# Third block's feed-forward in two phases, with seven block products per 2x2

## The chip, the cores and the metric

One core of one Trainium2 chip runs the whole program. The metric is the device time of one execution in microseconds. TensorE does the matmuls, VectorE and ScalarE the elementwise work, GpSimd some of it, and SyncE issues the transfers.

## The reference, cut to what matters

Three transformer-like blocks are applied one after another to x of shape (1, 1024 tokens, 1024 channels), all in float32. Only the end of the third block is touched: its output projection, its two layer norms and its feed-forward part.

```
def channel_mlp(h, w1, b1, w2, b2):            # w1 (1024, 4096), w2 (4096, 1024)
    return jnp.square(jax.nn.relu(h @ w1 + b1)) @ w2 + b2

x_new = deepnorm_update(x, y_l, g1, ln1_g, ln1_b)        # y_l = mixer output @ w_out
x_new = deepnorm_update(x_new, channel_mlp(modulate(x_new, sh2, sc2), w1, b1, w2, b2), g2, ln2_g, ln2_b)
# deepnorm_update(x, y, gate, g, b) = layer_norm(ALPHA * x + gate * y) * g + b
```

## The kernel before, in words

Activations are kept transposed, channels on the 128 partitions and tokens along the free axis, in two halves of 512 tokens. Each float32 product is made of three matmuls: weights and operand are each split into a rounded part (hi, made by ScalarE with a copy to the rounded type) and the rest (lo, made by VectorE with a subtraction), and hi·hi, hi·lo and lo·hi are added up in PSUM.

The stage is `chain_stage`, the same helper for all three blocks. In the third block it has N = 16 slabs of weights. A slab of the up weights (`in_w1_3`) gives 256 hidden channels: for two halves n and two row blocks m an `up_unit` does 8 x 3 matmuls of 128x512 (L1262 to L1264). ScalarE takes the result out of PSUM with bias and relu (L1457) and squares it to the hi part (L1459) and to the full square (L1461); VectorE subtracts for the lo part (L1717). A slab of the down weights (`in_w2_3`) takes these 256 hidden channels to all 1024 output channels: `down_half` does 8 output blocks of 2 x 3 matmuls for a half (L1301 to L1303), and VectorE adds each PSUM bank, times a gate, to the residual X (`drain`, L1754). So hidden values live only from one slab to the next, and never leave the chip's SBUF.

TensorE's order is written out by hand: up units of slab ch, then the down products of slab ch-1. `round_slab` (ScalarE, L1444) and `split_slab` (VectorE, L1699) prepare a whole slab of 128x2048 at once. SyncE loads a slab when the slot's last reader is done. The beginning of the stage holds the output projection and the two norms of each half (class `HalfNorm`, L823 on), with the first up units as filling. Its end is `down_last` (L1318 to L1320), then the last norm: mean, centre, squares, sums, root, scale, apply, for half 0 beside the last products and for half 1 alone at the very end.

Every engine works through its own instructions in the written order, and waits on semaphores.

## Time and profile before

| | |
|---|---|
| three runs, us | 3772.07, 3773.8, 3766.03; median 3772.07 |
| profiled execution, span from first to last instruction, us | 3772.8 |
| TensorE busy | 3631.5 us, 96%, 17008 matmuls |
| VectorE busy | 2237.2 us, 59% |
| ScalarE busy | 1233.3 us, 33% |
| GpSimd busy | 198.5 us, 5% |
| mean granted TensorE clock | 0.982 |
| moved by DMA | 225.29 MB, mean 60 GB/s |

Busy shares are means over the whole program. The profile gives no time for the profiled execution beside its span; the span lies 0.7 us above the median of the runs. In the rows, a matmul's own duration (about 0.39 us) is longer than the distance between two starts, because matmuls overlap.

### The profile page before, as it was taken

How to read it: one execution, taken by the hardware profiler on the slowest of the kernel's cores; microseconds unless marked ns; L12 is line 12 of the kernel's file. 1: busy time of each engine (PE TensorE's matmuls, PEld its weight loads, DVE VectorE, ACT ScalarE, POOL GpSimd, SP SyncE). 2: the span in 40 equal slices, each digit the busy share in tenths (PEclk: the TensorE clock that was granted, in tenths of full speed). 3: DMA queues.
4: the chain of work that ended last, by engine and by line, in shares of the span. 5: the costliest groups of instructions: out<-in, count | busy, mean ns of one | idle time of the engine just before them, and what ended most of it. 6: DMA issues, size and time to landing. Idle time of an engine off the chain costs nothing. (4 is left out here: it accounts for less than half of the span.)

```text
span 3772.8 us, 42367 instructions
## 1 busy us (share of the span) xinstructions
PE 3631.5 (96%) x17008; PEld 2942.7 (78%) x17008; DVE 2237.2 (59%) x3016; ACT 1233.3 (33%) x1789; POOL 198.5 (5%) x221
## 2 busy tenths in 40 slices
PE   8999999999998999999999999988998999999997
PEld 7977778888886877668788888867986778888885
DVE  4487577777777897454456555456355664444445
ACT  3344432222224413543322222244323462322223
POOL 0000000000003101230000000022100000000000
PEclk9999999999999999999999999999998999999999
DMA  3102111111111112120132222211222101111111
GB/s 126 45 1 90 34 45 51 51 51 50 40 51 56 62 56 53 39 90 34 45 119 94 90 90 90 89 62 46 63 59 94 41 25 65 45 45 45 45 60 53
DMA packets 68149, 225.29 MB, mean 60 GB/s; under 512 B 5565, under 2 KB 18237, under 8 KB 62706
## 3 DMA queue, kind: packets, MB, share of 16 engines
q1 hardware_dynamic: 67954, 222.58, 16.8%
q8 instruction: 136, 2.23, 0.2%
q14 instruction: 59, 0.48, 0.0%
HBM read 200.34 MB, written 13.70 MB: 57 GB/s over the span
## 5 line engine op out<-in xcount | busy, mean ns | idle before, releaser
L1262 PE MATMUL psum<-mixer_r,pairs_r 128*128 128x512 f32 x2016 | 793.8, 394 | 8.6 <-DVE gemm_input_r L1693 5.3
L1264 PE MATMUL psum<-mixer_r,pairs_r 128*128 128x512 f32 x2016 | 785.9, 390 | 0.0
L1263 PE MATMUL psum<-gemm_input_r,pairs_r 128*128 128x512 f32 x2016 | 785.8, 390 | 0.0
L1301 PE MATMUL psum<-hidden_r,pairs_r 128*128 128x512 f32 x1216 | 478.8, 394 | 13.0 <-DVE residual L1751 6.1
L1302 PE MATMUL psum<-hidden_r,pairs_r 128*128 128x512 f32 x1216 | 475.3, 391 | 0.0
L1303 PE MATMUL psum<-hidden_r,pairs_r 128*128 128x512 f32 x1216 | 475.2, 391 | 0.0
L1757 DVE TENSOR_TENSOR residual<-residual,psum 128x512 f32<-128x512 f32 x560 | 361.7, 682 | 171.4 <-PE psum L1303 144.3
L1262 PEld LDWEIGHTS psum<-mixer_r,pairs_r 128*128 128x128 f32 x2016 | 379.7, 188 | 93.3 <-issue 9.2
L1263 PEld LDWEIGHTS psum<-gemm_input_r,pairs_r 128*128 128x128 f32 x2016 | 379.7, 188 | 82.4 <-issue 4.1
L1264 PEld LDWEIGHTS psum<-mixer_r,pairs_r 128*128 128x128 f32 x2016 | 379.3, 188 | 79.2
L1699 DVE TENSOR_TENSOR pairs_r<-pairs,pairs_r 128x2048 fp32r<-128x2048 f32 (+1 forms) x108 | 223.4, 2070 | 276.5 <-ACT pairs_r L1444 276.5
L1444 ACT ACTIVATE pairs_r<-pairs 128x2048 fp32r<-128x2048 f32 (+1 forms) x108 | 187.2, 1736 | 595.6 <-DMA pairs<-in_w 376.2
L1754 DVE SCALAR_TENSOR_TENSOR residual<-psum,ada,residual 128x512 f32<-128x512 f32 x240 | 179.7, 750 | 175.5 <-PE psum L1303 166.6
L1301 PEld LDWEIGHTS psum<-hidden_r,pairs_r 128*128 128x128 f32 x1216 | 229.6, 189 | 65.1 <-DVE residual L1751 7.7
L1303 PEld LDWEIGHTS psum<-hidden_r,pairs_r 128*128 128x128 f32 x1216 | 229.5, 189 | 48.4
L1302 PEld LDWEIGHTS psum<-hidden_r,pairs_r 128*128 128x128 f32 x1216 | 229.6, 189 | 47.3 <-issue 0.2
L1717 DVE TENSOR_TENSOR hidden_r<-mixer,hidden_r 128x512 fp32r<-128x512 f32 x172 | 118.5, 690 | 103.4 <-ACT mixer L1461 82.8
L1452 ACT ACTIVATE conv_raw<-psum 128x512 f32<-128x512 f32 x88 | 52.5, 598 | 357.2 <-PE psum L1264 357.2
L2289 DVE SCALAR_TENSOR_TENSOR mixer<-scratch,params,mixer 128x1024 f32<-128x1024 f32 x120 | 157.2, 1310 | 4.1
L1726 DVE TENSOR_SCALAR mixer<-conv_raw,params 128x512 f32<-128x512 f32 x88 | 48.9, 555 | 155.5 <-ACT conv_raw L1452 155.4
L338 PE MATMUL psum<-gemm_input_r,weights_r 128*128 128x512 f32 x256 | 105.2, 411 | 10.9 <-DVE residual_r L638 10.9
L340 PE MATMUL psum<-gemm_input_r,weights_r 128*128 128x512 f32 x256 | 100.5, 392 | 0.0
(566 smaller groups left out, 5851.0 us busy)
## 6 DMA issues: line engine op xcount, KB each, us to landing
pairs<-in_w_up SPq DMA_DIRECT2D x38, 1024.0 KB, 6.9
pairs<-in_w SPq DMA_DIRECT2D x32, 1024.0 KB, 5.3
pairs<-in_w_down SPq DMA_DIRECT2D x16, 1024.0 KB, 5.2
norm_a<-in_w_ada SPq DMA_DIRECT2D x12, 1024.0 KB, 4.9
norm_b<-in_w_ada SPq DMA_DIRECT2D x12, 1024.0 KB, 5.0
pairs<-in_w_down SPq DMA_DIRECT2D x22, 512.0 KB, 3.5
pairs<-in_w_in SPq DMA_DIRECT2D x10, 1024.0 KB, 5.3
weight_slots<-in_w_in SPq DMA_DIRECT2D x9, 1024.0 KB, 4.9
```

Of the source, the lines that this page charges most:

```text
L1262: pe.matmul(out, w_hi[:, at], c.MR[:, k, halves[n]], start=k == 0, stop=False)
L1263: pe.matmul(out, w_hi[:, at], c.HR[:, k, halves[n]], start=False, stop=False)
L1264: mm = pe.matmul(out, w_lo[:, at], c.MR[:, k, halves[n]], start=False, stop=k == KT - 1)
L1301: pe.matmul(bank, hi, hid(0, ch, n, kd), start=kd == 0, stop=False)
L1302: pe.matmul(bank, lo, hid(0, ch, n, kd), start=False, stop=False)
L1303: mm = pe.matmul(bank, hi, hid(1, ch, n, kd), start=False, stop=kd == KD - 1)
L1444: act.activation(hi, src, ACT.Copy).then_inc(split_hi, 1)
L1699: dve.tensor_tensor(lo, src, hi.bitcast(F32), ALU.subtract).then_inc(split_ready, 1)
L1717: dve.tensor_tensor(hid(1, ch, n, m), mixed[n][:, m, :], hid(0, ch, n, m).bitcast(F32), ALU.subtract).then_inc(hid_ready, 1)
L1754: dve.scalar_tensor_tensor(out=x, in0=ps, scalar=gate(m), in1=x, op0=ALU.mult, op1=ALU.add).then_inc(down_drained, 1)
L1757: dve.tensor_tensor(x, x, ps, ALU.add).then_inc(down_drained, 1)
L2289: dve.scalar_tensor_tensor(out=out, in0=U[:, j:j + T], scalar=w, in1=out, op0=ALU.mult, op1=ALU.add).then_inc(taps, 1)
```

## The change

The third block calls `phased_stage` in place of `chain_stage`. Output projection, norms and the up products of the first three slabs stay as they were. After that:

- Up phase: 13 pairs. A pair is one slab (256 hidden channels) by all 1024 tokens, seen as a 2x2 of blocks in each operand, and made from seven block products in place of eight: 7 x 4 x 3 matmuls. Sums and differences of weight blocks are made by GpSimd, those of the operand once by VectorE. Four cells of results are put together by ScalarE (copy) and VectorE (add, square), and written to DRAM (`c.hidden`).
- Down phase: 20 groups. Groups 0 to 3 take 2+2 row blocks of hidden channels, groups 4 to 19 take 3+3; each group gives two output blocks by both halves from seven products of 2 x 3 or 3 x 3 matmuls. The weight sums are made by VectorE (`down_sums`), those of the hidden values by GpSimd (`operand_sums`), which are read back from DRAM. The operand blocks change after groups 3, 7, 11 and 15.
- Tail: the last 4 row blocks in the plain way, 16 x 4 x 3 matmuls.
- The residual is written to DRAM before, and added again during groups 8 to 15 (`add_residual`).

The core of the diff:

```diff
+DEPTHS = (2, 3, 3, 3, 3)
+BANK_OF = (0, 1, 0, 2, 0, 2, 0)
+OPENS = (True, True, False, True, False, False, False)
...
+            for i in range(PAIRS):                       # SyncE
+                keep(i, "11")
+                if i + 2 < PAIRS:
+                    sp.wait_ge(w_sums, 4 * (i + 2))
+                    sp.wait_ge(w_lo, SLABS + 3 * (i + 1) + 2)
+                    load_stage(i + 2)
+                if i == PAIRS - 1:
+                    sp.wait_ge(products, UP + 7 * (PAIRS - 1))
+                    load_block(0, "B22")
+                    load_block(0, "B12")
+                    load_down(0)
+                keep(i, "22")
+                keep(i, "21")
+                if i == PAIRS - 1:
+                    sp.wait_ge(products, UP + 7 * PAIRS)
+                    load_down(1)
+                keep(i, "12")
...
+            for g in range(GROUPS):                      # SyncE
+                q, j = divmod(g, 4)
+                if g:
+                    sp.wait_ge(products, DOWN + 7 * g)
+                    if g + 1 < GROUPS:
+                        load_down(g + 1)
+                if j == 0:
+                    sp.wait_ge(b_lo, 7 * (q + 1))
+                if q + 1 < CHUNKS_ and j < 2:
+                    for name in (("B22", "B12"), ("B11", "B21"))[j]:
+                        load_block(q + 1, name)
...
+            def down_group(g):                           # TensorE
+                q, j = divmod(g, 4)
+                h = depth(g)
+                pe.wait_ge(w_lo, SLABS + 3 * PAIRS + 2 * g + 1)
+                for r in range(7):
+                    if r == 2:
+                        pe.wait_ge(w_lo, SLABS + 3 * PAIRS + 2 * g + 2)
+                    if j == 0:
+                        pe.wait_ge(b_lo, 7 * q + r + 1)
...
+                    if g >= 2 and r in (0, 1, 3):
+                        drained(g - 2, {0: 6, 1: 1, 3: 5}[r])
+                    if r in (2, 4, 5, 6):
+                        drained(g, {2: 0, 4: 2, 5: 3, 6: 4}[r])
+                    product(PS[:, 3 * ((g + 1) % 2) + BANK_OF[r], :], r, h, down_high(g, DOWN_PLACE[r]), down_parts(g, DOWN_PLACE[r]),
+                            DOWN_HI, DOWN_LO).then_inc(products, 1)
...
+            for i in range(PAIRS):                       # ScalarE
+                if i + 1 < PAIRS:
+                    round_blocks(i + 1)
+                copy(i, "11", 0)
+                if i + 1 < PAIRS:
+                    round_sums(i + 1)
+                else:
+                    round_down(0, True)
+                copy(i, "21", 2)
+                if i == PAIRS - 1:
+                    round_operand(0, 0)
+                    round_operand(0, 1)
+                    round_operand(0, 2)
+                    round_down(0, False)
+                copy(i, "22", 3)
...
+            for g in range(GROUPS):                      # ScalarE
+                q, j = divmod(g, 4)
+                if q == 0:
+                    touch(g, 0)
+                if g + 1 < GROUPS and (g or q):
+                    round_down(g + 1, True)
+                if j == 3 and q + 1 < CHUNKS_:
+                    round_operand(q + 1, 0)
+                if q == 0:
+                    touch(g, 2)
+                if j == 3 and q + 1 < CHUNKS_:
+                    round_operand(q + 1, 1)
+                    round_operand(q + 1, 2)
+                if q == 0:
+                    touch(g, 3)
...
+                if g + 1 < GROUPS:
+                    round_down(g + 1, False)
+                if j == 3 and q + 1 < CHUNKS_:
+                    round_operand(q + 1, 3)
+                    round_operand(q + 1, 4)
+                    round_operand(q + 1, 5)
...
+            def operand_sums(q):                         # GpSimd
+                for name in b_landed:
+                    pool.wait_ge(b_landed[name], 16 * (q + 1))
+                pool.tensor_tensor(raw("T3"), raw("B22"), raw("B12"), ALU.subtract).then_inc(b_sums, 1)
+                pool.wait_ge(b_sums, 4 * q + 1)
+                pool.tensor_tensor(raw("T1"), raw("B12"), raw("B11"), ALU.subtract).then_inc(b_sums, 1)
+                pool.wait_ge(b_sums, 4 * q + 2)
+                pool.tensor_tensor(raw("T2"), raw("B22"), raw("T1"), ALU.subtract).then_inc(b_sums, 1)
+                pool.wait_ge(b_sums, 4 * q + 3)
+                pool.tensor_tensor(raw("T4"), raw("B21"), raw("T2"), ALU.subtract).then_inc(b_sums, 1)
...
+            def down_sums(g):                            # VectorE
+                dve.wait_ge(w2_landed[g % 2], 16 * (g // 2 + 1) + (0 if g % 2 else 16 * PAIRS))
+                part = lambda place: down_parts(g, place, 1, parts)
+                dve.tensor_tensor(part(4), part(0), part(2), ALU.subtract).then_inc(w_sums, 1)
+                dve.wait_ge(w_sums, 4 * PAIRS + 4 * g + 1)
+                dve.tensor_tensor(part(2), part(2), part(3), ALU.add).then_inc(w_sums, 1)
...
+            def low_operand(q, r):
+                h = DEPTHS[q]
+                dve.wait_ge(b_hi, 7 * q + r + 1)
+                if r in (0, 1, 6):
+                    dve.wait_ge(b_sums, 4 * (q + 1))
+                dve.tensor_tensor(block(*DOWN_LO[r], h), raw_block(q, OPERANDS[r]), block(*DOWN_HI[r], h).bitcast(F32),
+                                  ALU.subtract).then_inc(b_lo, 1)
...
+            for i in range(PAIRS):                       # VectorE
+                ahead = i + 1 < PAIRS
+                if ahead:
+                    low_blocks(i + 1, 0)
+                    low_blocks(i + 1, 1)
+                add(i, "11", 1)
+                if ahead:
+                    low_blocks(i + 1, 2)
+                else:
+                    low_operand(0, 0)
+                    low_operand(0, 1)
+                    down_sums(0)
+                    low_down(0, True)
+                    low_operand(0, 2)
+                    low_down(0, False)
+                add(i, "22", 4)
...
+            for g in range(GROUPS):                      # VectorE
+                q, j = divmod(g, 4)
+                switch = j == 3 and q + 1 < CHUNKS_
+                if g in READD:
+                    add_residual(g)
+                for r in range(7):
+                    if (g, r) in drain_at:
+                        drain(g, r)
+                    if switch and r:
+                        low_operand(q + 1, r - 1)
+                    if g + 1 < GROUPS and r == 1:
+                        down_sums(g + 1)
+                    if g + 1 < GROUPS and r == 2:
+                        low_down(g + 1, True)
+                    if g + 1 < GROUPS and r == 3:
+                        low_down(g + 1, False)
+                if switch:
+                    low_operand(q + 1, 6)
...
+                if g == GROUPS - 1:
+                    for e in range(2):
+                        dve.wait_ge(b_hi, 7 * CHUNKS_ + 3 + e)
+                        dve.tensor_tensor(tail_w_lo[e], tail_w_raw[e], tail_w_hi[e].bitcast(F32), ALU.subtract).then_inc(b_lo, 1)
+            b0, b1 = B
+            for m in range(KT):
+                drain_tail(0, m, b0)
+            b0.centre(dve)
+            b0.pairs(dve)
+            for m in range(4):
+                drain_tail(1, m, b1)
+            for k in range(KT):
+                b0.scale(dve, k)
+            for m in range(4, 8):
+                drain_tail(1, m, b1)
```

## Rows read from the trace of the kernel before

**Rows 1.** Windows of this stage, all engines: us, busy (count) each, PEclk, DMA share, GB/s
```profile
3200.00:3300.00 100.00, 100.00 (x443) 82.84 (x442) 43.76 (x48) 30.03 (x36) 0.00 (x0) 1.00 0.15 59
3500.00:3600.00 100.00, 100.00 (x443) 82.80 (x441) 41.37 (x47) 26.20 (x32) 0.00 (x0) 1.00 0.17 64
```

**Rows 2.** Window of TensorE (us, busy, count, PEclk), and two drains in a timeline of VectorE
```profile
3090.00:3680.00 590.00, 590.00 (x2604) 1.00 0.14 52
...
3670.24 0.75 DVE L1754 SCALAR_TENSOR_TENSOR residual<-psum,ada,residual 128x512 f32<-128x512 f32 x1 [0.61 <-PE psum L1303]
3671.60 0.75 DVE L1754 SCALAR_TENSOR_TENSOR residual<-psum,ada,residual 128x512 f32<-128x512 f32 x1 [0.61 <-PE psum L1303]
```

**Rows 3.** Waits of TensorE, 3060 to 3700 (last: 2920 to 3773): line, waited for, us, times, longest
```profile
PE psum L1301 <- DVE residual L1754: 2.4, 4, 1.4
PE psum L1318 <- DVE pairs_r L1699: 0.8, 1, 0.8
PE psum L1262 <- DVE gemm_input_r L1693: 5.3, 1, 5.3
```

**Rows 4.** Timeline of VectorE, single instructions and runs of several shapes
```profile
2699.91 0.42 DVE L3736 TENSOR_TENSOR pairs<-pairs,scratch 128x256 f32<-128x256 f32 x1
7.67 1.23 DVE L632 TENSOR_TENSOR weights_r<-weight_slots,weights_r 128x1024 fp32r<-128x1024 f32 x1 [6.29 <-ACT weights_r L507]
3682.92 2.29 DVE L1699 TENSOR_TENSOR pairs_r<-pairs,pairs_r 128x2048 fp32r<-128x2048 f32 x1 [6.49 <-ACT pairs_r L1444]
3695.84 0.75 DVE L1754 SCALAR_TENSOR_TENSOR residual<-psum,ada,residual 128x512 f32<-128x512 f32 x1 [0.63 <-PE psum L1320]
3696.62 0.69 DVE L900 TENSOR_TENSOR norm_a<-residual 128x512 f32<-128x512 f32 x1
```

**Rows 5.** Timeline of ScalarE, three shapes
```profile
3687.28 0.63 ACT L1459 ACTIVATE hidden_r<-mixer 128x512 fp32r<-128x512 f32 x1
29.53 1.05 ACT L507 ACTIVATE weights_r<-weight_slots 128x1024 fp32r<-128x1024 f32 x1
3688.48 1.90 ACT L1444 ACTIVATE pairs_r<-pairs 128x2048 fp32r<-128x2048 f32 x1
```

**Rows 6.** Timeline of GpSimd, adds and subtractions of three widths
```profile
2496.01 8.70 POOL L900 TENSOR_TENSOR norm_a<-norm_a,residual 128x512 f32<-128x512 f32 x6
2727.20 2.36 POOL L3291 TENSOR_TENSOR hidden_r<-mixer,hidden_r 128x1024 fp32r<-128x1024 f32 x1 [16.92 <-ACT hidden_r L3539]
```

**Rows 7.** Timeline of GpSimd and VectorE together, 2842 to 2848 and at 2548
```profile
2842.30 4.79 POOL L3291 TENSOR_TENSOR pairs_r<-pairs,pairs_r 128x2048 fp32r<-128x2048 f32 x1 [44.84 <-ACT pairs_r L3539]
2843.83 0.69 DVE L3794 TENSOR_TENSOR pairs<-psum,norm_b 128x512 f32<-128x512 f32 x1
2844.56 3.08 DVE L3796 TENSOR_TENSOR mixer<-mixer,pairs 128x512 f32<-128x512 f32 x1
2548.29 2.28 DVE L3699 TENSOR_TENSOR pairs_r<-pairs,pairs_r 128x2048 fp32r<-128x2048 f32 x1
2548.45 3.27 POOL L900 TENSOR_TENSOR norm_a<-residual 128x512 f32<-128x512 f32 x1 [15.92 <-DVE residual L920]
```

**Rows 8.** Transfers: issues, KB each, us from issue to landing (page; last: 0 to 40)
```profile
pairs<-in_w SPq DMA_DIRECT2D x32, 1024.0 KB, 5.3
pairs<-in_w_down SPq DMA_DIRECT2D x22, 512.0 KB, 3.5
residual<-in_x SPq DMA_DIRECT2D x4, 1024.0 KB, 11.3
```

**Rows 9.** Chain of waits and timeline of VectorE in the last 45 us
```profile
3732.06 3.43 PE psum L891 x8
3736.91 4.90 DVE L918 TENSOR_TENSOR residual<-residual,norm_a 128x512 f32<-128x512 f32 x8 [3.29 <-ACT norm_a L967]
3741.74 0.74 DVE L1754 SCALAR_TENSOR_TENSOR residual<-psum,ada,residual 128x512 f32<-128x512 f32 x1
3743.12 0.75 DVE L1754 SCALAR_TENSOR_TENSOR residual<-psum,ada,residual 128x512 f32<-128x512 f32 x1
```

**Rows 10.** Windows of TensorE: us, PE busy (count), PEclk, DMA share, GB/s
```profile
2918.00:2924.00 6.00, 0.72 (x5) 0.85 0.62 221
2924.00:2929.00 5.00, 5.00 (x12) 0.50 0.82 334
3060.00:3077.00 17.00, 14.61 (x53) 1.00 0.00 0
```

**Rows 11.** Waits of VectorE, 3075 to 3700: line, waited for, us, times, longest
```profile
DVE residual L1754 <- PE psum L1303: 166.6, 200, 4.1
DVE pairs_r L1699 <- ACT pairs_r L1444: 140.5, 29, 10.1
```

More of the change, by code:

```diff
@@ L89, in __init__ @@
         self.PWR = over("pairs_r", 36, [P, 12, T], F32R)
+        self.parts = over("parts", 36, [P, 15 * T])
+        self.parts_r = over("parts_r", 36, [P, 15 * T], F32R)
+        self.spread = over("spread", 8, [P, 28, T])
+        self.low_r = over("low_r", 16, [P, KT, T], F32R)
+        self.mid_r = over("mid_r", 24, [P, 4, T], F32R)
+        self.stage_rows = over("stage_rows", 26, [P, 2 * T])
+        self.tail_rows = over("tail_rows", 11, [P, 13, T])
+        self.tail_rows_r = over("tail_rows_r", 11, [P, 13, T], F32R)
+        self.tail_w = over("tail_w", 27, [P, 14, T])
+        self.tail_w_r = over("tail_w_r", 27, [P, 14, T], F32R)
+        self.hidden = nc.dram_tensor("hidden_rows", (P, 32, T), F32, kind="Internal").ap()
         self.conv_raw = over("conv_raw", 20, [P, 2, 2, HALF + 2])
@@ L827, in __init__ @@
     def __init__(self, c, s, n, spec, before, prev, x_ready, banks=None, squares_in=None, carried=(), paired=0,
-                 spilled=None, rest=None):
+                 spilled=None, rest=None, low_in=None):
+        self.low_in = low_in
         self.c, self.n, self.prev, self.x_ready = c, n, prev, x_ready
@@ L858, in hi, with lo @@
         return (self.c.XR if self.kind == "next" else self.c.MR)[:, k, self.half]
+    def lo(self, k):
+        return self.c.HR[:, k, self.half] if self.low_in is None else self.low_in(k)[:, self.half]
     def sq(self, k):
@@ L929, in low @@
         if self.lean:
-            dve.scalar_tensor_tensor(out=self.c.HR[:, k, self.half], in0=self.work(k), scalar=self.b(k),
+            dve.scalar_tensor_tensor(out=self.lo(k), in0=self.work(k), scalar=self.b(k),
                                      in1=self.hi(k).bitcast(F32), op0=ALU.add, op1=ALU.subtract).then_inc(self.s["lo_ready"], 1)
             return
-        dve.tensor_tensor(self.c.HR[:, k, self.half], self.work(k), self.hi(k).bitcast(F32),
+        dve.tensor_tensor(self.lo(k), self.work(k), self.hi(k).bitcast(F32),
                           ALU.subtract).then_inc(self.s["lo_ready"], 1)
@@ L2025, in _ @@
             drains(E, 1, range(4, 8), b1)
+            b1.centre(dve)
+            b1.pairs(dve)
+            for k in range(KT):
+                b1.scale(dve, k)
+    c.loads[:] = seen
+DEPTHS = (2, 3, 3, 3, 3)
+FIRST_ROW = [sum(2 * h for h in DEPTHS[:q]) for q in range(len(DEPTHS) + 1)]
+PHASE_SEMS = ("w_hi", "w_lo", "mix_hi", "mix_lo", "wo_done", "wo_drained", "products", "copied", "squared_y",
+              "spilled", "stage_landed", "w_sums", "added", "y_done", "t_raw", "t_hi", "t_lo", "w2_landed_1",
+              "b11_landed", "b21_landed", "b22_landed", "b12_landed", "b_sums", "b_hi", "b_lo", "x_landed",
+              "x_added")
@@ L3975, in build @@
                                              dict(kind="split", g=ada(32), b=ada(24), eps=ln_eps)],
+                                      offsets=(c.ada[:, 48:64:2], c.ada[:, 56:64:2], c.ada[:, 48:56:2]),
                                       last=dict(kind="x", g=g("ln2_g_3"), b=g("ln2_b_3"), eps=ln_eps), store=stored)),
@@ L3997, in wide_slab, with product_slabs @@
     return w.reshape(KT, P, HALF).transpose(1, 0, 2).reshape(P, KT * HALF)
+def product_slabs(w):
+    rows, out = w.reshape(-1, P, KT, P), []
+    for q, h in enumerate(DEPTHS):
+        for j in range(4):
+            of = rows[FIRST_ROW[q]:FIRST_ROW[q] + 2 * h][:, :, [j, j + 4], :]
+            out.append(of.transpose(1, 2, 0, 3).reshape(P, 4 * h * P))
+    return np.concatenate(out, axis=1)
 def down_slabs(w):
@@ L4065, in layouts @@
         "w1_3": pair_slabs(a["w1_3"][0]),
-        "w2_3": down_slabs(a["w2_3"][0]),
+        "w2_3": product_slabs(a["w2_3"][0]),
+        "w2_t_3": down_slabs(a["w2_3"][0][FIRST_ROW[-1] * P:]),
     }
```

656 lines of the change are left out of this document (655 added, 1 removed).

## The prediction

> **What bounds the kernel now.** I read the windows first: in the feed-forward of the third block TensorE is busy 100 of 100 us at full clock, VectorE about 43 and ScalarE 26 to 30, GpSimd not at all, and the transfers take 0.15 of the DMA engines [rows 1]. Then the timeline and a long window: between 3090 and 3680 there are 2604 matmuls in 590 us without a gap, one per 0.2266 us [rows 2]; I use 0.2267, since the drains behind every sixth are 1.36 us apart [rows 2]. Then TensorE's waits: 2.4 and 0.8 us in 640 [rows 3]. VectorE mostly waits for TensorE [rows 11]. So this stage costs its number of matmuls, and whatever takes its place is worth its matmuls less the waits it brings.
>
> **What is removed.** Before: 16 slabs x 192 = 3072 matmuls. After: 3 early slabs x 96 = 288; 13 pairs x 84 = 1092; 4 groups x 42 = 168; 16 groups x 63 = 1008; tail 192; together 2748. That is 324 fewer, x 0.2267 = **73.4 us**. These two waits, 3.2 us, sit at down products that are no longer there: 76.6 us of gain. This part is sure; the rest asks how much of it comes back as waits.
>
> **Prices used.** VectorE, two inputs: 0.42 us for 256 columns, 1.23 for 1024, 2.29 for 2048, so 0.55 for 384, 0.69 for 512, 0.96 for 768, 1.49 for 1280, 1.76 for 1536 (1.68 back to back), 2.16 for 1920; a drain 0.75 (0.67 back to back); a step that waits for the one before starts 0.03 after it [rows 4]. ScalarE: 0.63 for 512, 1.05 for 1024, 1.90 for 2048, so 0.85 for 768, 1.27 for 1280, 1.48 for 1536, 1.80 for 1920 [rows 5]. GpSimd: 1.45 per dependent 512-column step, 2.36 for 1024, 4.79 for 2048, so 3.5 for 1536 [rows 6, 7]. A transfer lands after 3.5 us for 512 KB and 5.3 for 1 MB, so 4.4 for 768 KB [rows 8]. A product of a pair is 12 matmuls, 2.72 us, of a group 6 (1.36) or 9 (2.04); a pair is 19.0, a group 9.5 or 14.3. From the last matmul's start to its reader I take 0.2 beyond the spacing, an estimate from matmuls of 0.39 us.
>
> **Up phase.** In a pair GpSimd needs 4 x 1.45 = 5.8 us, ScalarE about 6, VectorE about 8 of 19.0. The longest way, sums on GpSimd, then rounding (1.90), then the lo part (2.29), ends near 11.4 even where they wait for each other. Transfers: 1 MB issued near 8 lands near 13. Nothing is late; the cost is 0, all of it hidden by the other products of the pair. Before pair 0, VectorE's ten changes of the operand and ScalarE's four roundings fill the last six early units; I find 0.4 + 1.0 us of wait for the last copies: **1.4** (0 to 6).
>
> **Pair 12, where the phases meet.** Time 0 is its start. SyncE has `keep(12, "11")` ahead, which waits for product 1 (5.6) and two VectorE steps (7.1); only then go B22, B12 and the first down weights out. Three transfers of 512 KB in a row land near 11, 12.3 and 13.5. ScalarE waits in `round_down(0, True)` to 14.2, and the copy of cell 21 stands behind it: product 4, due at 10.9, starts at 14.9. GpSimd's `operand_sums(0)` are 4 x 2.5 from 12.3 to 22.5. VectorE waits for them in `low_operand(0, 0)`, then two operands (24.9), four sums (26.7); ScalarE's `round_down(0, False)` (28.0) and only then the copy of cell 22: product 5 starts at 28.7, product 6 at 31.4, end 34.1 against 19.0: **15.1** (8 to 22: with transfers of no length 3 us less for each of two waits; the upper end with GpSimd at 3 us a step).
>
> **A group without a change of operand, h = 3.** Weights for the next group can only be loaded when the group before is done, and land at 4.7. VectorE: drain 1 to 5.0, four sums x 0.58 to 7.35, drain 2 to 8.0 (needed for product 4 at 8.15), lo part 9.0, drain 3 9.65, second lo part 11.8, drain 4 12.45; product 6 was due at 12.2: 0.3 each. With the transfers of the operand blocks in the same queue I take 0.5 more in each of four groups: **4.4** with the rest. For h = 2 there are less products to hide the same: drain 4 ends at 9.8, due 8.2, so 1.75 for each of groups 1 and 2, 2.9 for group 0 (ScalarE and the late weights): **6.4**.
>
> **Groups 3, 7, 11, 15, where operands change.** Here VectorE also has seven `low_operand` of 1.7 = 11.8 us: 4.7 drains + 2.3 sums + 3.1 lo parts + 11.8 = 21.9 in a group of 14.3. In order: drain 1 5.0; `low_operand` of product 0 waits for ScalarE, which stood at the weights until 5.5 and rounds till 7.0: 8.8; sums 11.1; drain 2 11.8, so product 4 starts at 11.85 and not 8.15; operand 13.5, lo part 14.35, drain 3 15.05; product 5 then; operand 16.75, lo part 18.85, drain 4 19.5; product 6 19.55 to 21.6: +7.3. Operands 3 to 6 keep VectorE until 6.1 in the next group, whose product 2 needs drain 0 at 6.8 (+2.8), and the rest of that group then just keeps up: 10.3 with its own 0.3 wait. Group 3 has shorter products to hide it: 19.6 for 9.5, 13.0 with the next. Two of the next groups have `add_residual` at their head (1.3 each). 13.0 + 3 x 10.3 + 2.6 = **46.5** (20 to 65: the lower end is VectorE's load alone, 21.9 + 10 less 2 x 14.3 = 3.3 for each, and group 3).
>
> **GpSimd beside VectorE.** The trace shows that an elementwise VectorE step with two SBUF inputs does not run beside a two-input step of GpSimd: 512 columns took 3.08 us instead of 0.69 and ended 0.55 after GpSimd did, and GpSimd took 3.27 instead of 1.3 behind a 2.29 step; one with a PSUM input kept 0.69 [rows 7]. So drains go on, but sums and lo parts wait. `operand_sums` of 1536 columns are 4 x 3.6 = 14.5 us, in each of four chunks, from about 8.5 in group j = 1 into j = 2. The lo part of group j = 1 waits 2.4 us; in j = 2 the sums wait for up to two steps of 3.5, and come back as 3 to 4.2 us at product 4. Group 2, with its 9.5 us, loses 7.5. 7.5 + 5.5 + 2 x 6.7 = **26.4** (0 to 45). In the up phase the same waits stay under the cover of 19 us.
>
> **Tail.** The last weights' lo parts are put behind drain 6 of group 19: 15.2 + 2.3 = 17.5 against 14.3, so 3.3. At the end, root and `b0.scale` (1.4 + 4.9 us [rows 9]) had 48 matmuls, 10.9 us, beside them; now the second sums stand later, 5.4 us of matmuls remain, and four drains with adds (1.39 each [rows 9]) follow the scale: 5.0. **8.3** (2 to 12). Hidden values written and read are 34 MB more in 600 us, beside 50 GB/s used at 0.15 [rows 1]: nothing but the landing times above.
>
> **Clock.** After a wait of 5.3 us [rows 3] the granted clock was 0.50 for 5 us, 12 matmuls instead of 22 [rows 10]; after waits up to 1.4 us it stayed 1.00 [rows 10]. Pair 12 has an 11 us wait; the others are mostly under 4. I take two drops of 2.5: **5** (0 to 40).
>
> **Sum.** 1.4 + 15.1 + 4.4 + 6.4 + 46.5 + 26.4 + 8.3 + 5 = 113.5 back, 76.6 gained: 37 us slower. The profiled execution (3772.8) is the median within 0.8 us, so 3772.1 + 37 = **3809 us**.
>
> **Rivals.**
> (a) VectorE keeps up: between groups it has slack (10 of 14.3 us), and the order lets the backlog run out before a product waits. All that comes through drains 0, 2, 3 and 4 is 46.5 + 26.4 + 6.4 + 4.4 = 83.7 us; without it the time is 3725, with half of it 3767. It makes the change faster where the twenty groups together lose under 39 us, 2 us a group. For it: busy shares leave room everywhere [rows 1, 11]. Against: the queue is in order, drain 2 stands behind the sums and these behind a transfer, and nothing in the order changes that. 20%.
> (b) The mutual exclusion costs nothing, since GpSimd's steps fall where VectorE has only drains: 3809 - 26 = 3783. Against: its 14.5 us are longer than the gap between two groups' sums. 12%.
> (c) Loads land later than 4.7, being queued with each other (four of 1 MB together took 11.3 [rows 8]): each us goes almost whole into a group, 15 groups x 1.3 = 20: 3829. 12%.
> (d) The clock falls at each of the longer waits. There are about 16 of 2.5 us or more (two per change of operand, two per chunk for GpSimd), each with 2.4 us lost as in rows 10: 3809 - 5 + 38 = 3842. Against: 1.4 us didn't do it. 4%. The Trainium skill (TensorE: Matmul & The Clock Gate, HAM oscillation) says that idle gaps between bursts throttle the array again in each iteration; by that rule this case would be the forecast. The trace agrees with it for 5.3 us only.
>
> **How the numbers follow.** My own course has 52%, with a range of 3790 to 3832 from the ends of its largest terms taken against each other. The range that should hold 8 in 10 leaves out (a) beyond half (16%) and what lies beyond (d): 3764 to 3842. About 0.2% (7.5 us) can be told from no change. Faster by that is (a) from a little over half of its effect on, 16%. Within it are (a) at half effect (4%), (b) with milder changes of operand (5%) and the low end of my own course (2%), 11%. Slower is the rest, 73%.
>
> **What would show it.** TensorE's records in this stage down by 324, pairs of 19.0 us without a wait; a pair 12 near 34 us with waits of products 4 and 5 for ScalarE; groups 7, 11, 15 near 21.6 us and those behind them near 17, with TensorE waiting for VectorE's drains; VectorE sums of 384 columns at 3 us or more while GpSimd runs. Wrong would be: groups of 14.3 throughout (then a), down sums that never take longer than 0.6 us (then b), weights landing at 6 or later (then c), a mean clock well under 0.98 (then d).

## The result

| | us, median | lowest to highest | ratio to before, 95% interval |
|---|---|---|---|
| kernel before | 3772.94 | 3766.03 to 3780.87 | |
| changed kernel | 3810.11 | 3805.7 to 3814.66 | 1.0096 (1.0079 to 1.0112) |

The change makes the kernel 0.96% slower, 37.2 us by the medians; predicted were 3809 us and 37 us. The profiled executions are 40.1 us apart (3812.9 and 3772.8 us of span). Of these 4.9 lie ahead of everything that was edited: the wait of about 5 us before the third block's output projection [rows 3] ends at 2923.9 us before and at 2928.8 after, and in the kernels below between 2917.8 and 2928.8, with the same code in front of it. So 35.2 us lie behind that wait. In the 400 matmuls that follow it the work and its order are as before too, and the executions show two levels there: 9.8 to 9.9 us above 0.2267 us a matmul in the changed kernel and three of the others, 12.3 to 12.5 in the kernel before and the rest. By that the change costs some 37.7 us, close to the medians' 37.2.

These rows are from the page of the changed kernel. TensorE has 324 matmuls fewer (17008 before), VectorE 159 us more to do (2237.2 before), GpSimd 158:

```profile
span 3812.9 us, 42055 instructions
...
PE 3595.2 (94%) x16684; PEld 2901.2 (76%) x16684; DVE 2396.1 (63%) x3125; ACT 1271.7 (33%) x1779; POOL 356.4 (9%) x293
```

Its windows are, in the columns of rows 1, pairs 0 to 11, pair 12, groups 0 to 3, groups 4 to 16 and groups 17 to 19.

```profile
3113.00:3342.00 229.00, 228.38 (x1008) 189.21 (x1009) 119.63 (x109) 78.63 (x96) 77.61 (x48) 1.00 0.31 111
3342.00:3379.00 37.00, 24.64 (x88) 19.38 (x87) 14.65 (x18) 11.07 (x14) 9.43 (x4) 0.77 0.21 77
3379.00:3442.00 63.00, 42.78 (x168) 32.84 (x167) 40.30 (x42) 29.58 (x32) 14.05 (x4) 0.88 0.28 93
3442.00:3665.00 223.00, 189.23 (x758) 148.87 (x757) 181.82 (x184) 62.34 (x46) 49.12 (x12) 0.94 0.31 104
3665.00:3727.00 62.00, 59.72 (x254) 48.12 (x252) 44.93 (x52) 16.79 (x11) 0.00 (x0) 0.97 0.31 106
```

Where one engine was busy 100 of 100 us [rows 1] there is now a stage of three kinds: pairs that lose nothing, groups in which VectorE is busy 182 of 223 us and TensorE 189, and a middle where neither is. TensorE's waits say for whom, in pair 12, in the groups and in the tail:

```profile
PE psum L2359 <- ACT rows L2520: 12.4, 2, 8.0
...
PE psum L2359 <- DVE residual L2790: 53.2, 22, 8.3
PE psum L2359 <- ACT residual L2553: 3.1, 3, 1.8
...
PE psum L883 <- DVE norm_a L915: 6.5, 1, 6.5
...
PE psum L2430 <- DVE parts_r L2934: 3.1, 1, 3.1
```

L2790 is VectorE's drain, L2520 ScalarE's copy of a pair's cell. They replace the waits of 2.4 and 0.8 us in rows 3. VectorE's own waits in the groups show how little the loads have to do with it (L2753 is the first weight sum):

```profile
DVE residual L2790 <- PE psum L2361: 61.5, 47, 5.8
DVE low_r L2775 <- ACT mixer_r L2547: 9.7, 5, 2.6
...
DVE parts L2753 <- DMA parts<-in_w: 0.5, 2, 0.3
```

For each group, its length less its matmuls at 0.2267 us (9.5 us for groups 0 to 3, 14.3 for the others), worked out from the starts of the matmuls; "stage" is pair 12 to the last matmul of group 19, for which the matmuls alone need 285.7 us:

```
                p12   0    1    2    3    4    5    6    7    8    9    10   11   12   13   14   15   16   stage
changed         17.5  3.1  1.8  9.8 10.8  1.4  2.9  2.6  7.9  4.5  2.8  3.8  7.0  5.5  3.9  2.4  6.8  4.2  384.4
e1_sums_off     17.6  3.1  1.8  1.8 10.8  1.6  0.1  0.1  7.0  5.3  0.1  0.1  6.8  5.3  0.1  0.1  7.5  2.0  357.0
e2_handover     17.4  3.1  1.8  9.5  6.6  1.7  2.8  4.1  2.8  0.2  4.1  2.2  2.6  0.3  2.8  4.1  2.5  0.2  354.6
e3_meet          8.0  5.9  2.2  9.4 10.7  1.4  3.6  1.9  6.9  5.3  3.4  3.0  6.8  5.5  3.9  2.4  6.8  4.2  377.0
e6_order        17.1  1.1  0.0 10.1  5.4  3.7  0.4  7.5  1.3  2.8  2.4  8.1  1.3  2.8  2.2  8.2  1.3  1.9  363.7
e13_best         2.6  5.4  1.5  4.3  4.6  6.9  0.4  0.2  1.3  2.8  1.8  0.9  1.9  4.0  0.2  0.9  1.9  3.0  330.6
```

Where nothing near a group was edited it still moves by up to 1.8 us from one execution to the next, and the whole stage by about 3.

### The profile page after: what moved, and what is told of

Read it like the earlier page. It is cut to its first block and busy times, and to the rows that moved or that the text cites. A ratio compares the mean times of both kernels' runs of the same rounds, so it can differ in the third digit from the quotient of the medians.

```text
span 3812.9 us, 42055 instructions
## 1 busy us (share of the span) xinstructions
PE 3595.2 (94%) x16684; PEld 2901.2 (76%) x16684; DVE 2396.1 (63%) x3125; ACT 1271.7 (33%) x1779; POOL 356.4 (9%) x293
## 5 line engine op out<-in xcount | busy, mean ns | idle before, releaser
L1277 PE MATMUL psum<-mixer_r,pairs_r 128*128 128x512 f32 x1408 | 552.7, 393 | 3.4 <-ACT conv_raw L1467 1.7
L1279 PE MATMUL psum<-mixer_r,pairs_r 128*128 128x512 f32 x1408 | 548.4, 389 | 0.0
L1278 PE MATMUL psum<-gemm_input_r,pairs_r 128*128 128x512 f32 x1408 | 548.2, 389 | 0.0
L1316 PE MATMUL psum<-hidden_r,pairs_r 128*128 128x512 f32 x768 | 303.7, 395 | 10.7 <-DVE residual L1766 6.2
L1277 PEld LDWEIGHTS psum<-mixer_r,pairs_r 128*128 128x128 f32 x1408 | 264.8, 188 | 62.3 <-issue 7.3
L1278 PEld LDWEIGHTS psum<-gemm_input_r,pairs_r 128*128 128x128 f32 x1408 | 264.7, 188 | 56.7 <-issue 2.2
L1279 PEld LDWEIGHTS psum<-mixer_r,pairs_r 128*128 128x128 f32 x1408 | 264.6, 188 | 55.4
L1317 PE MATMUL psum<-hidden_r,pairs_r 128*128 128x512 f32 x768 | 300.9, 392 | 0.0
L1318 PE MATMUL psum<-hidden_r,pairs_r 128*128 128x512 f32 x768 | 300.9, 392 | 0.0
L1714 DVE TENSOR_TENSOR pairs_r<-pairs,pairs_r 128x1024 fp32r<-128x1024 f32 (+1 forms) x76 | 150.2, 1978 | 136.2 <-ACT pairs_r L1459 136.2
L1459 ACT ACTIVATE pairs_r<-pairs 128x1024 fp32r<-128x1024 f32 (+1 forms) x76 | 126.1, 1663 | 227.3 <-DMA pairs<-in_w_up 211.6
L2359 PE MATMUL psum<-mixer_r,parts_r 128*128 128x512 f32 x380 | 154.7, 407 | 41.6 <-DVE residual L2790 40.3
L1316 PEld LDWEIGHTS psum<-hidden_r,pairs_r 128*128 128x128 f32 x768 | 145.4, 189 | 43.7 <-DVE residual L1766 7.7
L2360 PE MATMUL psum<-gemm_input_r,parts_r 128*128 128x512 f32 x432 | 174.1, 403 | 0.0
L1318 PEld LDWEIGHTS psum<-hidden_r,pairs_r 128*128 128x128 f32 x768 | 145.4, 189 | 31.0
L1317 PEld LDWEIGHTS psum<-hidden_r,pairs_r 128*128 128x128 f32 x768 | 145.5, 189 | 29.7
L2361 PE MATMUL psum<-mixer_r,parts_r 128*128 128x512 f32 x380 | 152.9, 402 | 0.0
L2790 DVE SCALAR_TENSOR_TENSOR residual<-psum,ada,residual 128x512 f32<-128x512 f32 x124 | 92.2, 748 | 64.7 <-PE psum L2361 62.8
```

The costliest lines, as they stand in the source:

```text
L1277: pe.matmul(out, w_hi[:, at], c.MR[:, k, halves[n]], start=k == 0, stop=False)
L1278: pe.matmul(out, w_hi[:, at], c.HR[:, k, halves[n]], start=False, stop=False)
L1279: mm = pe.matmul(out, w_lo[:, at], c.MR[:, k, halves[n]], start=False, stop=k == KT - 1)
L1316: pe.matmul(bank, hi, hid(0, ch, n, kd), start=kd == 0, stop=False)
L1317: pe.matmul(bank, lo, hid(0, ch, n, kd), start=False, stop=False)
L1318: mm = pe.matmul(bank, hi, hid(1, ch, n, kd), start=False, stop=kd == KD - 1)
```

## The experiments

All start from the changed kernel. Differences in time are taken between ratios to the kernel before, since the runs were made on more than one occasion; each is uncertain by about 8 us, the stage lengths from the trace by about 3.

**GpSimd's sums left out.**

```diff
+                if q:
+                    for name in ("T3", "T1", "T2", "T4"):
+                        pool.memset(raw(name), 0.0).then_inc(b_sums, 1)
+                    return
```

> The changed kernel with GpSimd's four operand sums of chunks 1 to 4 replaced by four memsets of the same blocks (16 two-input steps of 1536 columns less; those sums are left out of what is computed). Theory (VectorE's weight sums and lo parts stand still while GpSimd runs a two-input step, and this comes back at product 4): groups 2, 6, 10 and 14 lose about 9.5, 2.7, 3.8 and 2.3 us less, the groups behind them some more, in all about 26 us: near 3784 us, 1.003 times the kernel before. Rival (the exclusion costs nothing, the same groups are late by VectorE's own work in order): no change, 3810 us, groups 2 and 6 as they were.

Measured 3780.18 us, 1.0021 (1.0011 to 1.003): 28 us faster. In the table it is the groups beside GpSimd's sums that change: 2, 5, 6, 9, 10, 13 and 14 lose 2.4 us together where they lost 28.2; of the others only group 16 differs by over a microsecond. The theory holds, and the rival falls. The timeline of the changed kernel at groups 5 and 6, VectorE first, then GpSimd, shows one of the four meetings:

```profile
3467.41 4.86 DVE L2766 TENSOR_TENSOR parts_r<-parts,parts_r 128x1920 fp32r<-128x1920 f32 x1
3472.19 1.40 DVE L2790 SCALAR_TENSOR_TENSOR residual<-psum,ada,residual 128x512 f32<-128x512 f32 x2
...
3479.48 0.75 DVE L2790 SCALAR_TENSOR_TENSOR residual<-psum,ada,residual 128x512 f32<-128x512 f32 x1 [1.29 <-PE psum L2361]
3480.15 3.05 DVE L2753 TENSOR_TENSOR parts<-parts 128x384 f32<-128x384 f32 x1
3483.23 0.56 DVE L2755 TENSOR_TENSOR parts<-parts 128x384 f32<-128x384 f32 x1
...
3466.75 3.50 POOL L2681 TENSOR_TENSOR spread<-parts,spread 128x1536 f32<-128x1536 f32 x1 [51.75 <-DMA parts<-hidden_rows]
3470.33 5.29 POOL L2683 TENSOR_TENSOR spread<-spread,parts 128x1536 f32<-128x1536 f32 x1
...
3479.28 3.51 POOL L2687 TENSOR_TENSOR spread<-parts,spread 128x1536 f32<-128x1536 f32 x1
```

The lo part took 4.86 us for 2.16 and the weight sum 3.05 for 0.55; GpSimd's second step took 5.29 for 3.5. Drains, with a PSUM input, kept 0.75 beside it.

**The handover cut to a third.** Edit, in `round_operand` and `low_operand` for q > 0:

```diff
+                cut = (lambda x: x) if q == 0 else (lambda x: x[:, h - 1:h, :])
```

> The changed kernel with the rounding and the lo part of each operand of chunks 1 to 4 done for one of its two or three row blocks only (the other blocks are left out of what is computed): every step, wait and order is kept, each step takes a third to a half of its time. Theory (VectorE's backlog of 11.8 us in groups 3, 7, 11 and 15 makes TensorE wait for the drains there and in the group behind): those eight groups lose 48 us together now and should lose about 20, so near 3781 us, 1.002 times the kernel before. Rival (these groups are late because loads land late or the clock is down, not because VectorE is full): no change, near 3810 us.

Measured 3779.22 us, 1.0019 (1.001 to 1.0029): 29 us faster. Groups 3, 4, 7, 8, 11, 12, 15 and 16 lose 16.9 us instead of 48.1, and the others differ by up to 1.7 either way. The work on the operands is the cause, not the loads or the clock. The edit shortens ScalarE's roundings as well as VectorE's lo parts, so it doesn't tell the two apart; that TensorE waits for VectorE's drains in these groups is in its waits above.

**The tail's order.**

```diff
+                    if g == GROUPS - 1 and r in (3, 4):
+                        e = r - 3
+                        dve.wait_ge(b_hi, 7 * CHUNKS_ + 3 + e)
+                        dve.tensor_tensor(tail_w_lo[e], tail_w_raw[e], tail_w_hi[e].bitcast(F32), ALU.subtract).then_inc(b_lo, 1)
...
-            down_tail_part(1, range(4, 8), 0)
             B[0].sums(pe)
+            down_tail_part(1, range(4, 8), 0)
             down_tail_part(1, range(4, 8), 1)
```

> The changed kernel with the lo parts of the last weights behind drains 3 and 4 of group 19 instead of behind drain 6, and the second sums of squares ahead of the first half of the tail's last down products instead of behind it. Same work. Theory: the wait of 3.1 us for these lo parts goes and that of 6.5 us for the normed output falls to about 2: 8 us less, near 3802 us. Rival: the lo parts delay drains 5 and 6 by as much and the end is set by the drains with their adds, not by the scale: no change within 2 us.

Measured 3797.45 us, 1.0067 (1.0052 to 1.0082): 11 us faster by the ratios. Of TensorE's waits in the tail two are left:

```profile
PE psum L906 <- DVE spread L927: 5.6, 1, 5.6
PE psum L883 <- DVE norm_a L915: 1.7, 1, 1.7
```

The 3.1 us are gone and 6.5 has become 1.7, which is 7.9. The tail gives more than that: from the last matmul of group 19 to the end of the execution it takes 75.4 us instead of 86.3 (the kernel before needs 74.7 for the same number of matmuls), so 10.9 us went, since the matmuls 0.43 us apart behind the waits went with them. That is the whole difference by the ratios. The theory holds, but its size was too small, and its rival falls.

**Pair 12's order.** The loads of B22, B12 and the first down weights ahead of `keep(12, "11")`; ScalarE's copies ahead of what waits for GpSimd; on VectorE:

```diff
-                    low_operand(0, 0)
-                    low_operand(0, 1)
                     down_sums(0)
                     low_down(0, True)
-                    low_operand(0, 2)
                     low_down(0, False)
                 add(i, "22", 4)
```

> The changed kernel with the steps of pair 12 in another order: the loads of B22, B12 and the first down weights ahead of keep(12, 11); ScalarE's copies of cells 21 and 22 ahead of what waits for GpSimd; VectorE's weight sums first and its operands behind the adds. Same work. Theory (pair 12 is late by 17.5 us because both copies stand behind waits for late loads and GpSimd's sums): pair 12 falls to about 20 us, the time by 15 to 17: near 3794 us. Half of it may come back in groups 0 to 2 if the operands become late there. Rival (the wait is for the data themselves, and moves to the first down product): pair 12 near 19, but the gap in front of group 0 grows by the same 15 us, no change.

Measured 3800.97 us, 1.0076 (1.0061 to 1.0091): 7.5 us faster, half of what was expected. Pair 12 lost 8.0 us instead of 17.5, and group 0 gave 2.8 of it back. ScalarE's copies no longer hold TensorE; what does now is VectorE's add for cell 22, which stands behind four weight sums that had become slow. VectorE in the timeline of this kernel:

```profile
3348.73 0.67 DVE L2754 TENSOR_TENSOR parts<-parts 128x256 f32<-128x256 f32 x1 [3.62 <-DMA parts<-in_w]
3349.43 2.50 DVE L2756 TENSOR_TENSOR parts<-parts 128x256 f32<-128x256 f32 x1
3351.97 2.50 DVE L2758 TENSOR_TENSOR parts<-parts 128x256 f32<-128x256 f32 x1
3354.51 2.45 DVE L2760 TENSOR_TENSOR parts<-parts 128x256 f32<-128x256 f32 x1
```

Three sums of 0.42 us took 2.5 each. GpSimd's four operand sums of 2.40 to 2.46 us ran from 3346.72 to 3356.67, and each of the last three sums of VectorE, which waits for the one before, ended just after a step of GpSimd did. In the changed kernel the four took 0.42 each, because VectorE itself stood until GpSimd was done. So the exclusion was hidden there by the bad order, and the better order met it.

**The waits filled.**

```diff
+            def fill(w_high, rows_, n):
+                for k in range(n):
+                    pe.matmul(PS[:, 6, :], w_high[:, 0:P], rows_[:, 0, :], start=True, stop=True, skip_group_check=True)
...
+                    if (g, r) in DOWN_FILL:
+                        fill(down_high(g, DOWN_PLACE[0]), block(*DOWN_HI[6 if j == 3 else 0], h), DOWN_FILL[g, r])
```

> The changed kernel, and 273 matmuls more, which write to an unused PSUM bank that nobody reads: they stand on TensorE's queue at the 23 places where it waits in pair 12 and groups 0 to 16 (50 in pair 12, the rest in the groups), in each place fewer than fit into the wait. In the records of the changed kernel the waits there are 68.6 us together, but pair and groups are 99 us longer than their matmuls at 0.2267 us: 30 us are matmuls 0.43 us apart behind the waits. Theory (the wait itself lowers the granted clock behind it): with the waits filled the clock stays up and most of the 30 us goes: near 3785 us, between 3780 and 3795. The same queues behind then make the waits a little longer. Rival (the lower clock has another cause, or the end is set by the other engines anyway, whose next step comes no earlier): within 3 us of 3810, or later by the matmuls that do not fit.

Measured 3806.48 us, 1.0091 (1.0075 to 1.0107): 2 us by the ratios, 3.6 by the medians, neither clear of the noise, and not 30. The matmuls added are 259, not 273: 50 in pair 12 and 209 in the groups. The granted clock did what the theory said. Its windows of pair 12 and the groups, in the columns of rows 1, had 0.77, 0.88 and 0.94 in the changed kernel:

```profile
3342.00:3379.00 37.00, 33.95 (x142) 27.24 (x141) 14.57 (x18) 12.23 (x16) 9.57 (x4) 0.95 0.22 76
3379.00:3442.00 63.00, 59.66 (x256) 47.15 (x255) 42.89 (x43) 30.73 (x33) 15.25 (x4) 1.00 0.30 104
3442.00:3665.00 223.00, 207.57 (x887) 165.65 (x886) 183.20 (x187) 61.91 (x46) 49.51 (x12) 0.99 0.29 104
```

The stage went from 384.4 to 378.2 us. The starts of the matmuls say where the rest stayed. In the changed kernel 72.6 us above 0.2267 a matmul lie in waits and 24.7 in matmuls 0.3 to 0.8 us apart (93 of them near 0.43, 19 us); the 30 us of the expectation count some 4 us too much, because a wait is counted there from the modelled end of the matmul before it. With the fillers the slow ones fell to 10.6 us, and waits and fillers together grew to 80.7. So some 14 us of slow matmuls went, 8 came back as waiting, and the lower clock cost about 6 us, uncertain by about 3. The rest was free: the time of the next drain is set on VectorE, whose load didn't change, and a faster TensorE only comes earlier to a longer wait. In group 7, which had three waits and one stretch of slow matmuls, 7.9 us became 6.8.

**The queues reordered in the groups.** VectorE's new order in a group where operands change, and in the one behind it (D drain, O and L operand, S weight sums, T1 and T2 lo parts, R residual):

```diff
+                    todo = [(D, 0), (O, 0), (D, 1), (D, 2), (O, 1), (D, 3), (S,), (T1,), (D, 4), (O, 2), (D, 5), (T2,), (D, 6)]
...
+                    todo = first + [(D, 1), (D, 2), (L, 5), (D, 3), (L, 6), (D, 4), (S,), (R,), (T1,), (D, 5), (T2,), (D, 6)]
```

> The changed kernel with VectorE's and ScalarE's steps inside the down groups in another order, the same work: a drain that the next product needs goes ahead of weight sums and lo parts; in the groups where operands change ScalarE rounds two operands before the weights, and VectorE mixes drains and lo parts; the added residual of groups 8 and 12 stands late. Theory (waits come from the order in the queue, not from the amount of work): groups 3, 7, 11, 15 and those behind lose about 30 us less, groups 0 to 2 and the groups with GpSimd's sums another 14: near 3766 us, 0.998 of the kernel before. Rival (VectorE is full in these groups): the waits move from one drain to another, less than 10 us gained.

Measured 3787.71 us, 1.0038 (1.0026 to 1.0051): 22 us faster, half of what was expected and twice what the rival allows. The groups of the handover and those behind, 48.1 before, lose 20.5: 27.6 of the 30 expected came. The second part failed: groups 2, 6, 10 and 14 lose 33.9 us where they lost 18.6. There GpSimd's operand sums met more of VectorE's weight sums than before: in group 6 two of them took 2.05 and 3.69 us for 0.55 each, where in the changed kernel one did (3.05). VectorE first, then GpSimd, in this kernel:

```profile
3466.94 2.05 DVE L2766 TENSOR_TENSOR parts<-parts 128x384 f32<-128x384 f32 x1
3469.02 3.69 DVE L2768 TENSOR_TENSOR parts<-parts 128x384 f32<-128x384 f32 x1
...
3465.06 3.50 POOL L2698 TENSOR_TENSOR spread<-parts,spread 128x1536 f32<-128x1536 f32 x1
3468.64 3.66 POOL L2700 TENSOR_TENSOR spread<-parts,spread 128x1536 f32<-128x1536 f32 x1
```

**Weight sums of most groups to GpSimd.**

```diff
+    def pool_sums(g):
+        return g >= 4 and (g - 1) % 4 != 2
```

> The changed kernel with the down weight sums of most groups from 4 on done by GpSimd instead of VectorE (not those that fall beside GpSimd's operand sums). Theory: VectorE has 2.3 us less in front of drain 2, but GpSimd's four dependent steps take about 4 us and still keep VectorE's two-input steps out: about 6 us gained, near 3804 us. Rival (the weight sums on VectorE are what delays the drains): each of the 12 groups gains 2 us, near 3786. Rival (GpSimd's steps take more from VectorE than they give): slower, near 3820.

Measured 3817.44 us, 1.0114 (1.0093 to 1.0136), and a stage of 385.0 us against 384.4: no gain. The median is 7 us slower, nearest to the second rival, but the intervals of the two ratios overlap, so a loss isn't shown. GpSimd's own chain of four takes 4.3 us for VectorE's 2.3, and VectorE's lo parts, which wait for it, then meet the operand sums. The timeline of this kernel shows GpSimd's last weight sum and first operand sum, then VectorE's two lo parts:

```profile
3456.02 1.01 POOL L2672 TENSOR_TENSOR parts<-parts 128x384 f32<-128x384 f32 x1
3456.99 3.48 POOL L2697 TENSOR_TENSOR spread<-parts,spread 128x1536 f32<-128x1536 f32 x1
...
3457.13 4.14 DVE L2776 TENSOR_TENSOR parts_r<-parts,parts_r 128x768 fp32r<-128x768 f32 x1 [1.73 <-POOL parts L2672]
3461.20 0.74 DVE L2800 SCALAR_TENSOR_TENSOR residual<-psum,ada,residual 128x512 f32<-128x512 f32 x1
3461.86 4.74 DVE L2776 TENSOR_TENSOR parts_r<-parts,parts_r 128x1920 fp32r<-128x1920 f32 x1
```

**Operand sums in pieces of 512 columns.**

```diff
+                    for k in range(DEPTHS[q]):
+                        a_ = [raw_block(q, name)[:, k, :] for name in (out, x, y)]
+                        op = pool.tensor_tensor(a_[0], a_[1], a_[2], ALU.subtract)
```

> The changed kernel with each of GpSimd's operand sums issued as two, three or four steps of 512 columns, one row block each, instead of one step over all of them. Same sums. Theory (VectorE's step waits until the GpSimd step that runs has ended, and then gets its turn): a wait is 1.3 us instead of up to 3.5, which is 0 to 5 us in all: 3805 to 3810. Rival (the two share the SBUF bandwidth, and it is the columns that count): no change. Rival (more turns for VectorE leave GpSimd late, and its last sum holds an operand): slower by up to 5.

Measured 3802.51 us, 1.008 (1.0065 to 1.0095), and a stage of 377.7 us: 6 to 7 us faster. Of these 4.5 lie in the groups beside GpSimd's sums, which lose 23.7 us where they lost 28.2, within the 0 to 5 expected; the rest is no more than a stage moves by itself. Groups 5, 9 and 13 fell to 0.6 us each, while 6, 10 and 14 rose to about 5. The same columns in shorter steps cost VectorE less, which speaks for the turn and against the bandwidth, on a difference not much above the noise.

**Operand sums at the groups' heads.**

```diff
+            for g in range(4 * (CHUNKS_ - 1)):
+                if g % 4:
+                    pool.wait_ge(products, DOWN + 7 * g)
+                    operand_sums(g // 4 + 1, ((), (0,), (1, 2), (3,))[g % 4])
```

> The changed kernel with GpSimd's operand sums of chunks 1 to 4 at other places, the same work in the same order on VectorE: instead of four in a row from the middle of a chunk's second group on, one starts with the second group, two with the third and one with the last, where VectorE has only drains to do for the first 5 us. Theory (GpSimd's steps cost only where a two-input SBUF step of VectorE is due, 29.9 us as the kernel without these sums showed): groups 1, 5, 9 and 13 lose nothing, groups 2, 6, 10 and 14 about 2 us where the second sum of two reaches into the weight sums (7.2 against 4.7 to 5.9), 15 to 20 us gained in all, near 3793 us. Rival (the cost is GpSimd's busy time as such, wherever it lies): no change, 3810 us. Rival (the sums are late now and hold the rounding for the last group): slower by up to 10.

Measured 3799.72 us, 1.0076 (1.0063 to 1.0089): 7.5 us by the ratios, 12.6 by the stage's length (371.8 us), less than the 15 to 20 expected. Groups 5 and 13 lose 0.1 and 1.9 us where they lost 2.9 and 3.9; the difference between them is the added residual, which in groups 9 to 15 is VectorE's first step and has two SBUF inputs. In this kernel's timeline it meets GpSimd's step in group 9, and drains 0 and 1 stand behind it (VectorE first, then GpSimd):

```profile
3523.65 3.77 DVE L2799 SCALAR_TENSOR_TENSOR residual<-spread,residual 128x1024 f32<-128x1024 f32 x1
3527.56 1.59 DVE L2790 SCALAR_TENSOR_TENSOR residual<-psum,ada,residual 128x512 f32<-128x512 f32 x2
...
3522.85 3.50 POOL L2685 TENSOR_TENSOR spread<-parts,spread 128x1536 f32<-128x1536 f32 x1 [35.80 <-PE psum L2361]
```

It took 3.77 us for 1.22 wherever it met a GpSimd step, and TensorE waited 1.6 to 2.0 us at product 2 in groups 9, 10, 11, 13, 14 and 15: some 10 us, of which 2.5 were there before. The rest is about what is missing. That VectorE "has only drains to do for the first 5 us" was wrong for these groups. The rival holds in so far as the place alone isn't enough; that GpSimd's busy time as such costs, it doesn't show.

**All orders together.** Pair 12's order with two weight sums on either side of the add, the groups' order, the sums at the heads with drain 2 ahead of the weight sums, the added residual (R) late in its group, and the tail's:

```diff
+                    todo = [(D, 0), (D, 1), (D, 2), (S,), (D, 3), (T1,), (D, 4), (T2,), (D, 5), (R,), (D, 6)]
```

> The changed kernel with the tail's order (12.7 us gained alone), the order of VectorE's and ScalarE's steps in the groups (22.4 alone), pair 12's order with the weight sums on both sides of the second add (9.1 alone with them ahead of it), GpSimd's operand sums at the groups' heads, and drain 2 ahead of the weight sums; the same work throughout. Theory (the changed kernel's 324 matmuls less are worth 73 us, and what took them back was the order of the queues): 22 + 12 + 9 to 13 + 15 to 25 gained, near 3745 us, 0.993 of the kernel before. Rival (VectorE is full over the chunks, and what is gained in one group is lost in the next): not below 3765.

Measured **3747.08 us, 0.9928 (0.9916 to 0.994)**: faster than the changed kernel by 63 us and than the kernel before by 27, with the same work. These are TensorE's waits in the stage:

```profile
PE psum L2362 <- DVE residual L2805: 13.9, 11, 4.1
PE psum L2362 <- DVE parts_r L2781: 10.4, 6, 4.1
PE psum L2362 <- issue: 2.0, 1, 2.0
```

With three smaller ones they are 27 us where there were 69. VectorE isn't full over the chunks, and the rival falls. Of the 63 us the stage gives 54 and the tail 11 (75.0 us from the last matmul of group 19 on). Half of what the stage still loses (22.7 of 45 us) stands in groups 0 to 4.

## Why the prediction was right

Its terms can be held against the traces one by one.

| term | predicted | measured | from |
|---|---|---|---|
| matmuls and old waits gone | -76.6 | -78.1 | 324 records fewer, pairs of 19.04 us; the old waits cost 4.7 with the matmuls behind them |
| up phase | 0 + 1.4 | 4.7 | 1.0 at pair 0, and 3.7 at L883: a wait of 2.2 and slower matmuls behind it |
| pair 12 | 15.1 | 17.5 | table |
| groups 0 to 2, plain | 6.4 | 6.7 | e1_sums_off |
| plain groups of three | 4.4 | 0.9 | e1_sums_off, groups 17 and 18 |
| operand changes | 46.5 | 48.1 | groups 3, 4, 7, 8, 11, 12, 15, 16 (46.3 in e1_sums_off) |
| GpSimd beside VectorE | 26.4 | 25.8 | 28.2 less 2.4 |
| tail | 8.3 | 11.6 | 86.3 us from the last matmul of group 19 on, 74.7 in the kernel before |
| clock | 5 | 6 (inside the other rows) | e11_filled |
| sum | 36.9 | 37.2 | 37.7 by the spans; 0.5 not placed |

The mechanism was right: three terms, pair 12, the operand changes and GpSimd beside VectorE, carry 91.4 of the 115.3 us that came back, and each measured within 2.4 us of its forecast. That the sum agrees within a microsecond is luck: the plain groups cost 3.5 us less than predicted, the tail 3.3 and the up phase 3.3 more, and these misses and the clock's cancel.

- **Pairs.** They lose nothing, as predicted; GpSimd's sums and VectorE's lo parts meet there too, under 19 us of matmuls.
- **Pair 12.** The prediction had product 4 start at 14.9 us and product 5 at 28.7; they start at 15.4 and 28.5. Weights landed at 12 to 14 us. In the timelines of TensorE and ScalarE:

```profile
3352.84 0.39 PE L2361 MATMUL psum<-residual_r,parts_r 128*128 128x512 f32 x1
3357.56 0.80 PE L2359 MATMUL psum<-residual_r,parts_r 128*128 128x512 f32 x1 [4.33 <-ACT rows L2520]
...
3370.72 0.80 PE L2359 MATMUL psum<-residual_r,parts_r 128*128 128x512 f32 x1 [8.02 <-ACT rows L2520]
3371.32 0.63 PE L2360 MATMUL psum<-gemm_input_r,parts_r 128*128 128x512 f32 x1
...
3356.30 0.63 ACT L2529 ACTIVATE parts_r<-parts 128x512 fp32r<-128x512 f32 x1 [10.51 <-DMA parts<-in_w]
3356.84 0.67 ACT L2520 ACTIVATE rows<-psum,params 128x512 f32<-128x512 f32 x1
...
3368.82 1.27 ACT L2532 ACTIVATE parts_r<-parts 128x1280 fp32r<-128x1280 f32 x1 [3.12 <-DVE parts L2759]
3370.00 0.67 ACT L2520 ACTIVATE rows<-psum,params 128x512 f32<-128x512 f32 x1
```

  Both copies stand right behind a rounding that waited, as the step says. The 2.4 us that were missing are matmuls behind the second wait, 0.43 us apart, which the prediction kept in its clock term.
- **Operand changes.** 46.5 was the right size, and its parts nearly so: groups 7, 11 and 15 lost 6.8 to 7.9 us (7.3 plus 0.3 predicted) and those behind 4.2 to 5.5 where 2.8 and twice 1.3 for the residual were laid down, groups 3 and 4 12.2 for 13.0.
- **GpSimd.** Group 2 loses 8.0 through it (7.5 predicted), the other three chunks 17.8 (18.9). The Trainium skill (SBUF — State Buffer, "SBUF: two separate sides") says that the port pair of VectorE and GpSimd is an exclusive lock, taken for a whole instruction by whichever starts first, and that a VectorE step with two SBUF inputs needs it; the trace agrees, with 4.86 for 2.16 us on one side and 5.29 for 3.5 on the other.
- **Plain groups.** This term failed: 4.4 us for transfers in one queue were not there. Weights landed after 4.3 us and VectorE waited 0.5 us for them in all; only operand blocks landed late (5.9). No wait of VectorE or TensorE is for them; GpSimd waited for them, and its first sum started 8.75 us into group 5, where 8.5 was predicted. That is rival (c), which falls:

```profile
parts<-in_w SPq DMA_DIRECT2D x16, 768.0 KB, 4.3
...
parts<-hidden_rows SPq DMA_DIRECT2D x12, 768.0 KB, 5.9
```

- **Early units.** 4.7 us against 1.4; the wait of 2.2 us for a normed row (L883), which was not in rows 3, was not foreseen.
- **Tail.** The wait for the last weights' lo parts was 3.3 us from start to start, as predicted, but some 1.7 us of slower matmuls stood behind it, and the end cost 6.5 us where 5.0 were predicted. With the up phase it was the term that was most too small; e5_tail took 10.9 us of it back.
- **Clock.** Rival (d) said that the clock falls at each longer wait. It did, at 12 waits between 1.8 and 8.3 us, with 6 to 10 matmuls 0.43 us apart behind each, though not at five of 2.1 to 3.2 us. These 93 matmuls took 19 us more than at 0.2267 us. Where another engine sets the next wait this isn't lost time: about 6 us came back when the waits were filled. The rival was mostly right on its mechanism and wrong on its price, and the forecast's own two drops of 2.5 us were a right sum from a wrong count, which is luck too. The Trainium skill (TensorE: Matmul & The Clock Gate, "HAM oscillation") puts the loss at half of the throttled time. By that, an estimate from the 93 matmuls of 0.43 us, it would be 20 us here, which agrees with the spacing in the records (19) and not with what e11_filled gave back.
- **Rivals (a) and (b).** VectorE had the room on average (182 of 223 us busy), and the order didn't let it use it; e13_best, which keeps every instruction, gets 54 us of stage back. (b) falls with e1_sums_off.

What GpSimd's sums still cost in the last kernel stays open, and so does what holds its groups 0 to 4; neither was tried.

## What to carry to other kernels

A saving of matmuls is worth its full price only while the engines behind can hand over inside the shorter product; before making the change, write each queue down in order, with its waits, and look for steps that the next product needs behind steps that it doesn't. Then reorder before moving work: here moving sums to GpSimd gained nothing, cutting its steps gained some 5 us and new orders alone 63. Don't price a tail by its waits alone: compare the time from the same matmul to the end in both kernels. Don't add up slow-clock time as a cost of its own where the waits are set by another engine.

## What the runs showed of the hardware

A two-input GpSimd step keeps VectorE's steps with two SBUF inputs out one by one: a chain of three sums of 0.42 us took 2.5 us each (e3_meet), and long GpSimd steps cost it 28.2 us where the same columns in steps of 512 cost 23.7 (e4_pieces). The granted clock could be held at 0.95 to 1.00 through 69 us of waits by matmuls that nobody reads, for a gain of 2 to 4 us in 3810, within the noise (e11_filled). The length of a wait doesn't decide by itself whether the clock falls behind it: it did after 1.8 us in group 8 and not after 3.2 us in group 7.
